# An expert layer: half of each result added at its own end, weights turned late, one-hots made mid-turn

## The reference, cut to what matters

```
combine = jnp.sum(jax.nn.one_hot(top_idx, N_EXPERTS, dtype=jnp.float32) * top_w[..., None], axis=1)
y = jnp.zeros_like(t)
for e in range(N_EXPERTS):
    hid = jax.nn.silu(t @ w_gate[e]) * (t @ w_up[e])
    y = y + combine[:, e:e + 1] * (hid @ w_down[e])
...
x = layer_norm(DEEPNORM_ALPHA * x + g2 * f, ln2_g[l], ln2_b[l])
```

## Time and profile before

| what | value |
|---|---|
| median of 3 runs | 2008.28 us (2001.38 to 2009.51) |
| the profiled execution | 1999.2 us, span 1997.5 us |
| PE, PE loads, DVE, ACT busy | 89%, 48%, 25%, 8% of the span |
| read from HBM | 624.46 MB, 314 GB/s over the span |
| part 1 ends, turns begin | 862 us |
| starts of the gathers | 864.2, 1180.3, 1455.4, 1709.1 us |
| mean granted clock of PE | 0.955 |

### The profile page before, as it was taken

The page is one execution under the profiler, slowest core; times in us unless marked ns, Lnnn a source line. Parts: engine busy times, 40 slices in busy tenths (PEclk is TensorE's granted clock), DMA queues, the critical chain, the costliest instruction groups (busy, mean ns, idle before and its releaser), DMA issues.

```text
span 1997.5 us, 21265 instructions
## 1 busy us (share of the span) xinstructions
PE 1773.3 (89%) x8790; PEld 960.5 (48%) x8791; DVE 508.5 (25%) x938; ACT 163.3 (8%) x340; POOL 2.5 (0%) x9
## 2 busy tenths in 40 slices
PE   5897999999999999969788879899889888798994
PEld 2346888688888864444322243322242222432221
DVE  0522536655445011320211110211201111111114
ACT  0000013100000000130000010000020000200000
POOL 0000000000000000000000000000000000000000
PEclk8998999999999999989999989999989999899997
DMA  9888774687766544306689986899979999598995
GB/s 394 356 323 289 299 322 192 257 344 295 323 275 277 220 190 168 139 31 253 242 334 427 425 347 274 337 426 427 427 299 427 426 425 428 209 368 364 427 426 219
DMA packets 49256, 630.68 MB, mean 316 GB/s; under 512 B 5615, under 2 KB 8080, under 8 KB 10152
## 3 DMA queue, kind: packets, MB, share of 16 engines
q1 hardware_dynamic: 47512, 621.58, 75.3%
q10 hardware_dynamic: 1552, 6.57, 0.8%
HBM read 624.46 MB, written 3.67 MB: 314 GB/s over the span
## 4 chain that ended last, share of the span: by engine, by line
PE 75%; DMA 14%; DVE 4%; issue 4%; SPq 2%; ACT 1%; ACTq 0%; DVEq 0%
PE bank L750 38%; PE bank L552 23%; PE bank L563 9%; DMA ring<-in_w_down 6%; DMA ring<-in_w_up_gate 4%; PE bank L575 2%; DMA region_a<-in_x_T 2%; DMA ring<-in_w_in 1%; DMA ring<-in_ada_w 1%; SPq L409 1%; DVE region_a L1577 1%; PE bank L570 1%; DVE ada_rows L1286 1%; PE bank L620 0%; PE bank L783 0%
## 5 line engine op out<-in xcount | busy, mean ns | idle before, releaser
L552 PE MATMUL bank<-ring,region_b 128*64 128x512 f32 x2048 | 479.2, 622 | 67.6 <-issue 54.8
L750 PE MATMUL bank<-region_a,ring 128*128 128x256 f32 x1792 | 393.5, 381 | 12.6 <-DMA ring<-in_w_in 12.6
L750 PEld LDWEIGHTS bank<-region_a,ring 128*128 128x128 f32 x1792 | 341.7, 191 | 62.9 <-DMA ring<-in_w_in 13.0
L552 PEld LDWEIGHTS bank<-ring,region_b 128*64 128x64 f32 x2048 | 148.6, 143 | 372.3 <-issue 364.0
L563 PE MATMUL bank<-ring,region_f 128*64 128x512 f32 (+1 forms) x1536 | 258.7, 524 | 30.6 <-DMA ring<-in_w_down 24.3
L1286 DVE SCALAR_TENSOR_TENSOR ada_rows<-ring,condT,ada_rows 128x512 f32<-128x512 f32 x293 | 220.3, 752 | 10.4 <-DMA ring<-in_ada_w 0.5
L563 PEld LDWEIGHTS bank<-ring,region_f 128*64 128x64 f32 (+1 forms) x1536 | 87.3, 128 | 186.9 <-issue 136.4
L1577 DVE TENSOR_TENSOR region_a<-bank,region_a 128x512 f32<-128x512 f32 x128 | 79.5, 684 | 259.6 <-PE bank L575 258.7
L750 PE MATMUL bank<-ring,region_a 128*128 128x512 f32 x256 | 119.9, 626 | 6.2 <-DVE region_a L1263 6.2
L750 PE MATMUL bank<-ring,region_b 128*128 128x512 f32 x256 | 110.3, 592 | 1.3 <-issue 1.3
L750 PE MATMUL bank<-region_e,region_x 128*128 128x256 f32 x256 | 65.2, 422 | 30.8 <-DVE region_e L1622 30.8
(11 more groups left out here) (165 smaller groups left out, 669.6 us busy)
## 6 DMA issues: line engine op xcount, KB each, us to landing
ring<-in_w_up_gate SPq DMA_DIRECT2D x128, 2048.0 KB, 17.6
ring<-in_w_down SPq DMA_DIRECT2D x64, 2048.0 KB, 15.6
ring<-in_ada_w SPq DMA_DIRECT2D x48, 2048.0 KB, 13.1
ring<-in_w_in SPq DMA_DIRECT2D x34, 2048.0 KB, 17.5
ring<-in_w_branch SPq DMA_DIRECT2D x8, 2048.0 KB, 17.6
ring<-in_w_out SPq DMA_DIRECT2D x8, 2048.0 KB, 11.3
ring<-in_w_in SPq DMA_DIRECT2D x4, 1024.0 KB, 4.9
region_a<-in_x_T ACTq DMA_DIRECT2D x4, 512.0 KB, 26.4
```

Of the source, the lines that this page charges most:

```text
L552: last = nc.tensor.matmul(bank_of(x, j)[n * c:n * c + n, 0:2 * m], tokens(x, 8 * half + k), w[:, k, :, m * c:m * c + m], start=(half == 0 ...
L750: return nc.tensor.matmul(out, lhsT, rhs, start=start, stop=stop)
```

## The change

It moves work inside the expert part and adds none:

- `add_up(le, 0)` is now done by every expert for itself, after its last `down` unit; half 1 goes to the next expert, in a plain one behind the transpose of `hid[1]`, between the two halves of the first `down` unit. A turn's last expert still does both at its end.
- In a plain expert `turn_weights` stands behind the transpose of `hid[1]` and uses bank 4. The wait behind it is gone for experts with extras too; the next user of bank 5 waits instead, counted by `turn_no`.
- PE's counter signals for the extras that an expert lacks stand ahead of the last `down` unit.
- DVE makes the marks of the first turn ahead of the loop, and those of the next turn in the third expert of each turn (`mark_tokens`). The last turn makes none, so on DVE it is written out behind a loop of three. The other engines keep a loop of four.

```
             def add_up(of, q):
+                if of == le and q == 0:
+                    pe.wait_ge(t_taken, ne * 3 + 1 + turn_no(xs, "weights"))
                 pe.wait_ge(y_ready, (g * GRP + of) * 2 + 3 + q)
...
                 pe.wait_ge(t_taken, ne * 3 + 1)
-                turn(hotw.rearrange("p a n -> p (a n)")).then_inc(t_full, 1)
-                pe.wait_ge(t_taken, ne * 3 + 2)
+                turn(hotw.rearrange("p a n -> p (a n)"), bank=5 if xs else 4).then_inc(t_full, 1)
...
             if xs:
                 if le > 0:
-                    add_up(le - 1, 0)
                     add_up(le - 1, 1)
...
-            if not xs and le > 0:
-                add_up(le - 1, 0)
...
-            if not xs:
-                turn_weights()
...
-            if not xs and le > 0:
-                add_up(le - 1, 1)
             pe.wait_ge(hid_ready, ne * 2 + 1)
...
             turn(hid[1]).then_inc(t_full, 1)
-            pe.wait_ge(t_taken, ne * 3 + 4)
+            if not xs:
+                turn_weights()
+                if le > 0:
+                    add_up(le - 1, 1)
+            pe.wait_ge(t_taken, ne * 3 + 1 + turn_no(xs, 1))
...
             down(0, 1, last).then_inc(y_full, 1)
+            add_up(le, 0)
             if le == GRP - 1:
-                add_up(le, 0)
                 add_up(le, 1)
...
+            def mark_tokens(g, first):
+                for le in range(GRP):
+                    for a in range(TT):
+                        ins = dve.tensor_scalar(hot[:, a, le, :], slots[:, 0:CAP], chosen(expert_at(g, first + le), a), None,
+                                                ALU.is_equal)
+                ins.then_inc(hot_ready, 1)
...
+                    if more and le == GRP // 2:
+                        mark_tokens(g, GRP)
...
+            mark_tokens(0, 0)
+            with dve.Fori(0, NE // GRP - 1) as g:
+                turn_of_experts(g, True)
+            turn_of_experts(NE // GRP - 1, False)
```

More of the change, by code:

```diff
@@ L161, with turn_no @@
 HALVES = len(HALF_NO)
+def turn_no(xs, what):
+    return 1 + (("weights", 0, 1) if xs else (0, 1, "weights")).index(what)
 BANK_JOBS = GATHER_JOBS + 2 * GRP
@@ L566, in down, with turn @@
                 return last
-            def turn(src, blocks=2):
+            def turn(src, blocks=2, bank=5):
                 for b in range(blocks):
-                    last = nc.tensor.transpose(psum[5][:, b * P:(b + 1) * P], src[:, b * P:(b + 1) * P], ident)
+                    cols = slice(b * P, (b + 1) * P)
+                    last = nc.tensor.transpose(psum[bank][:, cols], src[:, cols], ident)
                 return last
@@ L735, in expert_pe @@
             extras("F")
+            for x in EXTRA:
+                if x not in xs:
+                    pe.sem_inc(x_pe[x], pe_count(x, "all"))
             down(0, 1, first).then_inc(half_used, 1)
@@ L1041, in expert_act @@
                 act.activation(silu_g[j], psum[j][:, 0:256], ACT.Silu).then_inc(h_silu, 1)
-                if not xs and j == 0:
-                    take_weights()
                 extras(two)
-                act.wait_ge(t_full, ne * 3 + 2 + j)
+                act.wait_ge(t_full, ne * 3 + turn_no(xs, j))
                 take_turned(0, j).then_inc(t_taken, 1)
+            if not xs:
+                take_weights()
             for x in EXTRA:
@@ L1493, in slot_no, with chosen, weight, turn_of_experts @@
                 return slots[:, first:first + n].rearrange("p (o s) -> p o s", o=1).to_broadcast([P, copies, n])
[L1495 to L1499, removed]
-                    return wts.rearrange("p (a e) -> p a e", a=TT)[:, a, bass.ds(e, 1)]
+            def chosen(e, a):
+                return place.rearrange("p (a e) -> p a e", a=TT)[:, a, bass.ds(e, 1)]
+            def weight(e, a):
+                return wts.rearrange("p (a e) -> p a e", a=TT)[:, a, bass.ds(e, 1)]
+            def mark_tokens(g, first):
[4 more added lines that the diff above has]
+                ins.then_inc(hot_ready, 1)
+            def turn_of_experts(g, more):
                 def expert_dve(ne, e, le, xs):
@@ L1600, in expert_dve @@
                         extras(one)
-                        if not xs and le > 0:
-                            add_up(le - 1, j)
                         dve.wait_ge(h_silu, ne * 2 + 1 + j)
@@ L1606, in expert_dve @@
                             extras(two)
+                    if not xs and le > 0:
+                        add_up(le - 1, 1)
                     scale(0)
@@ L1620, in _ @@
                 for le in range(GRP):
-                    for a in range(TT):
-                        ins = dve.tensor_scalar(hot[:, a, le, :], slots[:, 0:CAP], chosen(expert_at(g, le), a), None,
-                                                ALU.is_equal)
-                ins.then_inc(hot_ready, 1)
-                for le in range(GRP):
                     count = dve.value_load(counts[0:1, bass.ds(expert_at(g, le), 1)], min_val=0, max_val=T)
                     ne, e = g * GRP + le, expert_at(g, le)
+                    if more and le == GRP // 2:
+                        mark_tokens(g, GRP)
                     for a in range(TT):
```

10 lines of the change are left out of this document (3 added, 7 removed).

## The result

The changed kernel takes 2008.1 us (median of 20 runs) where the kernel before takes 2000.0 us (20 runs). The ratio is 1.0033, with a 95% interval of 1.002 to 1.0046: 6.6 us slower (4 to 9), which is within 0.5%.

What follows compares the result with a forecast made beforehand. It took DMA to bound long stretches and PE's path between them to count. Turns of + 1.2, + 2.3, - 3.2 and + 2.7 summed to + 3.0 us: 2011.3 on the median, range 1999.5 to 2016.5.

Steps and rivals of the forecast that it cites:

- What bounds the kernel: Expert part: DMA sets the time in long stretches; edits count only on PE's way between them, where DMA rests.
- (1) One-hots: Turn starts: with marks made mid-turn, PE's gather starts earlier in turns 2 to 4; 9.25 us gained.
- (2) The wait: Experts with extras, turns 1, 2, 4: PE no longer waits 0.75 us for ScalarE's copy; 2.25 us gained.
- (3) The tail: First experts of turns 1, 2, 4: eight add passes now precede the jump, 1.92 us each; 5.8 us lost.
- (4) The branch: First expert's end, turns 2 and 4: longer code makes the cheap branch far; net 8.7 us lost, bounds 0 and 12.
- The jump behind it starts later, when the ring is full: Jump into the second expert, turns 2 and 4: 5.70 us for 6.43 and 6.52, saving 0.73 and 0.82.
- The PE gap: Sign after the first expert of turns 2 and 4: two long branches and 9 us of PE gap, not 4.25.
- A: First expert's end, turns 2 and 4: branch stays cheap, its lengthening costs nothing; 2002.6 us, chance 0.22.
- B: Turn starts: the gather gains nothing, another PE wait takes the marks' time; 2020.5 us, chance 0.04.
- C: Behind the jump into the second expert: PE runs dry awaiting a packet, up to 2.5 us in three turns; 2018.8, chance 0.07.
- D: Turn starts and expert ends: branches nearly free, only marks cost, gather starts as adds end; 1989.0 us, chance 0.02.
- The rule that the prediction weighed: PE's instruction memory: 2048 instructions would keep a 562 target cheap; a window of two 16 KiB blocks would not.

Runs made afterwards that it cites:

- place 129: Kernel before with only the order of the adds changed, branch after the first expert at slot 129 of its 256-instruction packet: 1.0133, 26.6 us slower.
- place 59: Loop head pinned so that branch stands at slot 59 of its packet: changed kernel 0.9953 against the kernel before; order of adds alone 1.0042.
- place 75: Slot of the first expert's end branch in the kernel before (2000.0 us); the hint version, also without the wait and with mid-turn one-hots, keeps it: 1979.0 us.
- places 20 to 51: Only the loop head moved: changed kernel with the branch at slot 20, 1.0031; kernel before at slot 34, 1.0025, and slot 51, 1.0012.
- place 51: Kernel before with no work changed, loop head moved so the first expert's end branch stands at slot 51 of its packet: 1.0012, no difference.
- place 34: Kernel before with no work changed, loop head moved so the first expert's end branch stands at slot 34 of its packet: 1.0025, 5.0 us slower.

## Why the prediction held, and where its steps were off

The forecast was 2011.3 us and no change that can be told; 2008.1 was measured. That these lie 3.2 us apart is luck in part: the base, a median of 3 runs, stood 8.3 us above the 2000.0 us of 20 runs, and the rise of 3.0 us was 6.6. The direction of every step was right, and three sizes were wrong, which partly cancelled.

- **What bounds the kernel.** Right: DMA's stretches kept their lengths (178 us for 179, and 238 for 239 in turn 3), and the differences lie between them.
- **(1) One-hots.** Predicted 9.25 us; 9.2 us (4.8 to 13.6) measured alone, with 3.0 us per turn in the trace. In the changed kernel 11.0 us were gained at the three gathers, since the counters that step 1 doesn't name were also moved ahead of the last products: 0.6 us per turn (4.02 for 4.62 us from the last add-up to the backward branch).
- **(2) The wait.** Predicted 2.25 us, measured 7.8 (4.6 to 11.0). The idle time was sized rightly in one execution at a good clock (in the changed kernel L629, once L620, follows without any); that the wait goes with a lower granted clock in part of the runs was not in the step. It was the largest miss by its ratio.
- **(3) The tail.** Predicted 5.8 us; with the branch short, the order alone costs 8.4 us (4.6 to 12.2), of which the traces show 1.5 and 1.8 us in turns 2 and 4. The sequencer's head start, which I took to leave the tail uncovered, was rightly read. No step had turn 1's longer first jump; it adds some 2 us at place 129 and nothing at place 59.
- **(4) The branch.** The mechanism was right: the branch is short at place 75 with 417 ahead and long at 129 with 433, and moving the loop alone takes it away or brings it. The size was wrong: 8.7 us predicted, 16 us measured (changed kernel against place 59), 13 us of it in these four branches and the rest not located. The long branches cost 6.3 and 6.1 us more than the short ones and not 5.1 and 5.2. The step that failed is "The jump behind it starts later, when the ring is full: I take turn 1's 5.70 us": in turn 2 the jump began at 1279.4 and took 7.32 us, 0.9 more than before, and DMA still ran until about 1283.5. The DMA row of the changed kernel from 1262 to 1290 us, in 40 slices of 0.7 us:

```profile
DMA  9989899899200093989999898999942000000000
```

The working also has turn 1's two durations the wrong way round: by the starts the branch that is short elsewhere took 5.70 us (992.3 to 998.0) and the jump behind it 5.47. The sum of 8.7 us is the same either way. The bound of 12 us was too low as well. The PE gap, forecast at 9 us, was 10.73.

- **Turn 3** gained 2.2 us and not what the one-hots gave elsewhere. The new order, with the weights' and counters' new places, costs 1.7 us there (251.39 at place 59 against 249.70 for the one-hots without the wait). Over that stretch a down unit's half takes 25.4 us from issue to landing for 22.2, and from the gather to the last add-up 97.7 MB come and not 96.8, so later transfers share the lines earlier. That is read from two traces, not tested, and stays open.
- **Rivals.** A (the branch stays cheap) would have needed other luck with the place: the run at place 59 is that world, at 9.4 us faster. B, C and D are out: the gather gained, PE has no gap in the 96 products behind the jump of turn 2, and no long branch took less than 3.3 us.

In parts, this is one-hots and wait - 15.8, order + 6.4 (place 59 against one-hots and no wait), branches + 16, together + 6.6; that holds by construction, since each part is the difference of two neighbours. The test is the three separate runs, one-hots - 9.2, wait - 7.8, order at place 129 + 26.6: + 9.6 us, which their intervals (4.4, 3.2 and 4.6 us either way) allow for 6.6.

The rule that the prediction weighed came out as it took it. A branch 433 instructions ahead takes 0.38 us or 6.6 by its place alone, so PE here doesn't have 2048 instructions loaded ahead. The Trainium skill (Runtime: NRT & Kernel Launch, Instruction fetch mechanics) names a window of two pages, and a branch out of it has to be fetched. The traces agree (0.3 to 0.5 us inside it at places 59 to 75, 3.6 to 6.6 us outside), and add that the second page has to have landed: at places 20 to 51 the target lies inside and the branch took 1.0 to 6.4 us.

## What to carry to other kernels

When an edit makes the code of one engine longer or shorter, look at its branches in the trace, not only at its work: one branch that leaves the loaded packets, run twice, cost here as much as all the stalls that the edit removed, and pinning the loop's head got it back without touching the work. Price an idle time by several runs and their granted clocks, not by one trace: a wait of 0.75 us three times was worth 7.8 us. When a jump is made earlier or later, ask whether the transfers are running at that moment, since its price rises from 3.3 to 4.3 us to 5.2 to 7.7 with them.

## What the runs showed of the hardware

- A far branch on PE took 3.3 to 4.3 us when DMA was silent at its start (64 branches in 14 traces), and 5.2 to 7.7 us when the transfers ran (229; 6.61 us at 382 GB/s). The same jump of turn 2, met earlier in the kernel with the hint, went from 3.66 to 6.12 us.
- A branch into the next packet ended about 1.4 us behind that packet's landing, or took 0.31 to 0.49 us where more time had gone by (places 59 to 75 without the hint): 1.0 to 1.4 us at place 51, 1.1 to 2.1 us at place 34. This fits a fetch ahead that starts only when the sequencer enters the packet before.
- A hint at the head of the loop, some 29,000 instructions of code ahead of its branch by my count, made the backward branch 0.37 to 0.46 us where it was 6.1 to 6.6.
- Three idle times of 0.7 to 1.3 us within 6 us went with a fall of the granted clock for part of the time from the 2.4 GHz level to that of 1.2 GHz, in three of seven profiled executions; with the first of the three idle times gone, none of seven profiled executions fell there, and no execution at all had a mean clock under 0.953.
